# Two transformer blocks: the first quarter of the modulation is summed by TensorE on four column tiles

## The reference

```python
mod = (c @ w_mod[l] + b_mod[l]).reshape(B, N_MOD, D)
shift_m, scale_m, gate_m = mod[:, 0, None], mod[:, 1, None], mod[:, 2, None]
...
h = rms_norm(x, g_pre_mix[l]) * (1 + scale_m) + shift_m
proj = h @ w_in[l]
```

## Time and profile before

| | us |
|---|---|
| median of 3 runs (2346.0 to 2348.29) | 2347.09 |
| the profiled execution | 2344.91 |
| its span, first to last instruction | 2343.2 |
| TensorE busy | 2323.7 |
| VectorE busy | 1672.4 |
| ScalarE busy | 1132.8 |

### The profile page before, as it was taken

How to read it: one execution, slowest core, us unless ns; L and a number is a source line. 1 busy time by engine, 2 the same in 40 slices (tenths; PEclk the granted TensorE clock), 3 DMA queues, 4 the chain that set the end, 5 groups by cost and what they waited for, 6 DMA issues and landing times.

```text
span 2343.2 us, 31060 instructions
## 1 busy us (share of the span) xinstructions
PE 2323.7 (99%) x10584; PEld 1920.3 (82%) x10584; DVE 1672.4 (71%) x2121; ACT 1132.8 (48%) x1439; POOL 450.1 (19%) x878
## 2 busy tenths in 40 slices
PE   8999999999999999999999999999999999999998
PEld 7888788887878888888888888888888888888887
DVE  6998899999876666655544466676765577888764
ACT  4544546543564444444444455444744444544654
POOL 0001001333002112112100001111121135686310
PEclk9999999999999999999999999999999999999999
DMA  9986469999957877866655657666566666665564
GB/s 391 397 321 202 156 235 372 350 345 367 361 185 253 263 252 239 271 228 200 230 195 193 193 169 233 212 219 215 183 210 216 200 212 200 198 199 190 187 210 154
DMA packets 175642, 562.62 MB, mean 240 GB/s; under 512 B 30464, under 2 KB 34848, under 8 KB 174880
## 3 DMA queue, kind: packets, MB, share of 16 engines
q1 hardware_dynamic: 145584, 528.28, 65.9%
q0 software_dynamic: 27136, 23.91, 3.5%
q10 hardware_dynamic: 2800, 8.81, 1.1%
HBM read 534.91 MB, written 2.11 MB: 229 GB/s over the span
## 4 chain that ended last, share of the span: by engine, by line
PE 92%; DVE 4%; issue 2%; DMA 1%; ACT 0%; SPq 0%; ACTq 0%; DVEq 0%
PE acc L2524 28%; PE acc L2525 28%; PE acc L2531 28%; DVE macc L1526 1%; DVE lo L1490 1%; PE tb L3111 1%; PE tb L2609 1%; DMA start_raw<-in_wa_dram 1%; PE tb L2524 1%; PE tb L2525 1%; PE tb L2531 1%; PE tb L3114 0%; PE tb L2796 0%; PE acc L2582 0%; PE acc L2584 0%
## 5 line engine op out<-in xcount | busy, mean ns | idle before, releaser
L1490 DVE TENSOR_TENSOR lo<-raw,hi 128x1024 fp32r<-128x1024 f32 x809 | 970.7, 1209 | 532.5 <-ACT hi L760 529.2
L760 ACT ACTIVATE hi<-raw 128x1024 fp32r<-128x1024 f32 x809 | 843.6, 1048 | 971.2 <-PE acc L2531 681.5
L2524 PE MATMUL acc<-hi,Hh 128*128 128x512 f32 x1928 | 759.9, 394 | 1.1 <-issue 0.9
L2525 PE MATMUL acc<-hi,Hl 128*128 128x512 f32 x1928 | 751.0, 390 | 0.0
L2531 PE MATMUL acc<-lo,Hh 128*128 128x512 f32 x1928 | 515.8, 389 | 1.1 <-DVE lo L1490 1.1
L2524 PEld LDWEIGHTS acc<-hi,Hh 128*128 128x128 f32 x1928 | 362.1, 188 | 78.3 <-issue 4.0
L2531 PEld LDWEIGHTS acc<-lo,Hh 128*128 128x128 f32 x1928 | 361.9, 188 | 77.2 <-DVE lo L1490 1.6
L2525 PEld LDWEIGHTS acc<-hi,Hl 128*128 128x128 f32 x1928 | 362.2, 188 | 74.9 <-issue 1.4
L2524 PE MATMUL acc<-hi,hbh 128*128 128x512 f32 x512 | 202.7, 396 | 0.0
L2525 PE MATMUL acc<-hi,hbl 128*128 128x512 f32 x512 | 199.6, 390 | 0.0
L675 POOL DMA_DIRECT2D tok<-sgt x176 | 86.2, 498 | 495.1 <-DVE sgt L1616 381.5
(11 more groups left out here) (398 smaller groups left out, 2336.1 us busy)
## 6 DMA issues: line engine op xcount, KB each, us to landing
raw<-in_wa_dram SPq DMA_DIRECT2D x680, 512.0 KB, 4.4
late_raw<-in_wa_dram SPq DMA_DIRECT2D x96, 512.0 KB, 6.3
raw<-in_wb_dram SPq DMA_DIRECT2D x96, 512.0 KB, 4.2
start_raw<-in_wa_dram SPq DMA_DIRECT2D x64, 512.0 KB, 7.6
raw<-in_wc_dram SPq DMA_DIRECT2D x64, 512.0 KB, 4.2
tok<-sgt POOLq DMA_DIRECT2D x416, 32.0 KB, 4.5
landed<-sgt POOLq DMA_DIRECT2D x192, 32.0 KB, 4.0
pt_landed<-att_parts POOLq DMA_DIRECT2D x192, 12.0 KB, 3.0
```

Of the source, the lines that this page charges most:

```text
L760: act.activation(hi[:, s, 0:n], raw[:, r, 0:n], ACT.Copy).then_inc(hi_ready, 1)
L1490: dve.tensor_tensor(lo[:, s, 0:n], raw[:, r, 0:n], hi[:, s, 0:n].bitcast(F32), ALU.subtract)\
L2524: pe.matmul(dst(tt), a, hi[:, s, w], start=first and i == 0, stop=False)
L2525: pe.matmul(dst(tt), b, hi[:, s, w], start=False, stop=False)
```

## The change

TensorE sums tiles 0 to 7, 12, 14 and 15 itself. It uses its array as four column tiles of 32 columns: the stationary operand of each is one column of c spread over 32, the moving operand four blocks of 32 columns of the raw tile, and the result gathers in one bank of `tb`, repeated on 32 partitions of each quarter. One 128x128 transpose by VectorE brings it into the wanted layout. VectorE keeps tiles 8 to 11 and 13 and hands its sum in `macc` to TensorE, which adds it into the same bank. VectorE also norms the second half of the tokens and copies half of the turned blocks, which ScalarE did. The fillers before the first tile fall from 76 to 34, and those before the fourth unit from 20 to 8. Unit 3 is multiplied unsplit too, from the scaled slices in `sgt`. The second quarter's tiles are requested from unit 6 instead of unit 4. ScalarE asks for the tables after the scaling for the third quarter. Semaphores become one for each column tile or sender.

```diff
-START_PE = (5, 8)
-FIRST_UNITS = 3
+START_PE = tuple(range(8)) + (12, 14, 15)
+QUADRANTS = 4
+FIRST_UNITS = 4
+TURN_BANKS = 0, 1, 2, 0, 1, 2, 2, 2
...
+HALF_SUMS = HALF_TILES, START_PE.index(KD - 1) + 2
...
-START_LEAD, START_LAST = 4, 16
+START_LEAD, START_LAST = 6, 16
...
-                        sp.wait_ge(mod_summed, START_PE.index(free_of) + 1)
+                        for j in range(QUADRANTS):
+                            sp.wait_ge(mod_summed[j], START_PE.index(free_of) + 1)
...
-            for unit in range(FIRST_UNITS):
+            for unit in range(FIRST_UNITS - 1):
                 load(wa[RING_MODS + unit])
                 load_start(HALF_TILES + unit)
...
             for n in (slice(0, D // 2), slice(D // 2, D)):
-                for tt in range(TT):
-                    act.activation(xn[:, tt, n], x[:, tt, n], ACT.Copy, scale=rstd[:, tt:tt + 1]).then_inc(start_normed, 1)
-            for k in range(KD // 2):
...
+                act.activation(xn[:, 0, n], x[:, 0, n], ACT.Copy, scale=rstd[:, 0:1]).then_inc(start_normed[0], 1)
+            for k in range(0, 6, 2):
...
-            split_to(RING)
+            for b in range(3):
+                act.wait_ge(tb_free[b], 1 + TURN_BANKS.count(b))
             scale_second()
-            at = P
-            for dst, n in ((ropeC, TT * HD), (ropeS, TT * HD), (iropeC, TT * IROPE), (iropeS, TT * IROPE)):
-                act.dma_start(dst[:], table_in[:, at:at + n].rearrange("p (a b) -> p a b", a=TT)).then_inc(const_in, 16)
-                at += n
-            act.dma_start(mask1[:], mask1_in).then_inc(const_in, 16)
...
             split_to(2 * PHASE - 1)
             scale_in(2)
...
+            def start_turned(k):
+
+                dve.wait_ge(tr_copy, k + 1)
+                dve.tensor_copy(xnT[:, 2 * k:2 * k + 2, :], tb[:, TURN_BANKS[k], :].rearrange("p (k t) -> p k t", k=2))\
+                    .then_inc(tb_free[TURN_BANKS[k]], 1)
...
             def start_pair_input(i):
...
-                dve.wait_ge(mod_based, i + 1)
-                dve.wait_ge(mod_read, 2 + i + 1)
-                ins = dve.tensor_tensor(pair(modfm[:, 0:8]), pair(tb[:, 3, 0:8]), pair(modfm[:, 0:8]), ALU.add)
-                ins.then_inc(mod_taken, 1)
+                sums = macc[:, 0, i * P:(i + 1) * P]
+                for j in range(QUADRANTS):
+                    dve.wait_ge(mod_summed[j], HALF_SUMS[i])
+                chain(dve.transpose(sums, tb[:, 3, T + i * P:T + (i + 1) * P]))
+                dve.tensor_tensor(pair(modfm[:, 0:8]), sums.rearrange("p (s k r) -> p s k r", s=2, r=32)[:, :, :, 0],
+                                  pair(vec("b_mod", 0, 8)), ALU.add).then_inc(mod_taken, 1)
...
+            def start_second():
+
+                for j in range(2, 4):
+                    dve.tensor_scalar(h_now[:, j, :], xnT[:, j, :], fA[:, j:j + 1], modfm[:, 4 + j:5 + j], ALU.mult, ALU.add)\
+                        .then_inc(start_scaled[1], 1)
+                dve.wait_ge(start_scaled[1], 2)
+                dve.wait_ge(in_hi, 2)
+                dve.tensor_tensor(Hl[:, 2:4, :], h_now[:, 2:4, :], Hh[:, 2:4, :].bitcast(F32), ALU.subtract).then_inc(in_split, 1)
...
             dve.wait_ge(fm_loaded, 16)
-            for m in range(HALF_TILES):
-                if m not in START_PE:
-                    start_rows(m)
-                if m == 0:
-                    dve.wait_ge(ssq_ready, c.up("ssq"))
-                    rms(D)
...
+            dve.wait_ge(ssq_ready, c.up("ssq"))
+            rms(D)
+            for n in (slice(0, D // 2), slice(D // 2, D)):
+                dve.tensor_scalar(xn[:, 1, n], x[:, 1, n], rstd[:, 1:2], None, ALU.mult).then_inc(start_normed[1], 1)
+            for k in (1, 3, 5):
+                start_turned(k)
             start_pair_input(0)
+            start_turned(6)
...
             for m in range(HALF_TILES, KD):
                 if m not in START_PE:
                     start_rows(m)
-                if m == HALF_TILES + 2:
-                    start_base(1)
-            dve.wait_ge(in_hi, 1)
-            dve.tensor_tensor(Hl[:, 0:2, :], xnT[:, 0:2, :], Hh[:, 0:2, :].bitcast(F32), ALU.subtract).then_inc(in_split, 1)
-            split_to(RING)
+                if m == HALF_TILES + 1:
+                    start_turned(7)
+                if m == HALF_TILES + 3:
+                    dve.wait_ge(in_hi, 1)
+                    dve.tensor_tensor(Hl[:, 0:2, :], xnT[:, 0:2, :], Hh[:, 0:2, :].bitcast(F32), ALU.subtract).then_inc(in_split, 1)
...
             start_pair_input(1)
-            start_pair(1)
+            start_second()
...
+            def column_sums(half, src, gain, first, last):
+
+                blocks = src.rearrange("p (i f) -> p i f", f=P)
+                at = slice(T + half * P, T + (half + 1) * P)
+                for j in range(QUADRANTS):
+                    quadrant = slice(32 * j, 32 * j + 32)
+                    ins = pe.matmul(tb[quadrant, 3, at].rearrange("p (i r) -> p i r", r=32), gain.to_broadcast([P, 32]),
+                                    blocks[:, :, quadrant], start=first, stop=last, tile_position=(0, 32 * j))
+                    yield j, ins
...
             def sum_rows(m):
...
+                for r in range(2):
+                    for j, ins in column_sums(half, start_raw[s][:, r * N:(r + 1) * N], vec("c", m % HALF_TILES * 2 + r),
+                                              m in (0, START_PE[HALF_TILES]) and r == 0, m in (HALF_TILES - 1, KD - 1) and r == 1):
+                        if r == 1:
+                            ins.then_inc(mod_summed[j], 1)
+
+            def sum_second():
+
+                pe.wait_ge(mod_used, start_used(KD))
+                for j, ins in column_sums(1, macc[:, 0, N:], ones[:], False, False):
+                    ins.then_inc(mod_summed[j], 1)
...
-            turn_ident(76)
+            turn_ident(34)
             pe.wait_ge(fm_loaded, 16)
...
+            for m in range(3):
+                sum_rows(m)
+                turn_ident(4)
+            for k in range(3):
+                turn_xn(k)
+            for m in range(3, 6):
+                sum_rows(m)
+                turn_xn(m)
+            sum_rows(6)
+            turn_ident(4)
+            sum_rows(7)
+            turn_xn(6)
...
-            for dst in (lambda tt: tb[:, tt, :], *first_parts):
-                unsplit_unit(dst)
-            pe.wait_ge(mod_based, 2)
-            sum_half(1)
-            for _ in range(20):
+            unsplit_unit(latent_parts, lambda k: xnT[:, k, :], start_scaled[0], True)
+            turn_xn(7)
+            unsplit_unit(first_parts[0], lambda k: xnT[:, k, :], start_scaled[0], True)
+            unsplit_unit(first_parts[1], lambda k: xnT[:, k, :], start_scaled[0], True)
+            fill(2)
+            sum_rows(12)
+            sum_rows(14)
+            sum_second()
+            sum_rows(15)
+            for _ in range(8):
                 pe.transpose(tb[:, 2, 0:P], ident[:], ident[:])
+            unsplit_unit(latent_parts, lambda k: sgt[:].rearrange("p t (k n) -> p (t k) n", k=2)[:, 2 + k, :], start_scaled[1], False)
             pe.wait_ge(in_split, 2)
-            latent_unit(0, 1)
             for dst in first_parts:
                 unit(dst, Hh, Hl, 2, 2, N, False, True)
```

More of the change, by code:

```diff
@@ L364, in two_blocks @@
         mod_used = sem("mod_used")
-        mod_summed = sem("mod_summed")
-        mod_based = sem("mod_based")
-        start_normed = sem("start_normed")
-        start_scaled = sem("start_scaled")
+        mod_summed = [sem(f"mod_summed{j}") for j in range(QUADRANTS)]
+        start_normed = [sem(f"start_normed{tt}") for tt in range(TT)]
+        start_scaled = [sem(f"start_scaled{i}") for i in range(2)]
         memory_set = sem("memory_set")
@@ L584, in _ @@
                 load_start(m)
-            for unit in range(FIRST_UNITS):
+            for unit in range(FIRST_UNITS - 1):
                 load(wa[RING_MODS + unit])
                 load_start(HALF_TILES + unit)
-            for m in range(HALF_TILES + FIRST_UNITS, KD):
+            for m in range(HALF_TILES + FIRST_UNITS - 1, KD):
                 load_start(m)
-            for unit in range(FIRST_UNITS, FFN0):
+            for unit in range(FIRST_UNITS - 1, FFN0):
                 for q, kt in START_AT.get(unit, ()):
@@ L925, in _ @@
             scale_in(2)
+            at = P
+            for dst, n in ((ropeC, TT * HD), (ropeS, TT * HD), (iropeC, TT * IROPE), (iropeS, TT * IROPE)):
+                act.dma_start(dst[:], table_in[:, at:at + n].rearrange("p (a b) -> p a b", a=TT)).then_inc(const_in, 16)
+                at += n
+            act.dma_start(mask1[:], mask1_in).then_inc(const_in, 16)
             split_to(3 * PHASE - 1)
@@ L1676, in start_rows @@
             def start_rows(m):
-                half, s = m // HALF_TILES, m % START_SLOTS
-                dst = macc[:, 0, half * N:(half + 1) * N]
-                first = m == (0, HALF_TILES + 1)[half]
+                s = m % START_SLOTS
```

(42 more changed lines are left out.)

43 lines of the change are left out of this document (17 added, 26 removed).

## The result

The changed kernel takes 2352.19 us (median of 11 runs, 2349.64 to 2353.8) against 2345.82 for the kernel before beside it (11 runs): ratio 1.0027, 95% interval 1.0019 to 1.0035. It is slower by 6.4 us, outside the range of 2342.3 to 2349. The profiled execution took 2351.61 us with a span of 2349.8.

What follows compares the result with a forecast made beforehand. TensorE, busy 99% of the span, was taken as the bound. Restart -4.9 plus 0.7 for the unsplit unit gave -4.1, plus 1.2 given back to DMA -2.9: median 2344.2 us, range 2342.3 to 2349.

Steps and rivals of the forecast that it cites:

- (a): First quarter's start: TensorE sums tiles 0 to 7 at 0.6 us each, unsplit units start at 22.0 instead of 25.04.
- (b): First quarter's second half: tiles 12, 14, 15 on TensorE; it resumes at 36.4 instead of 41.29, 4.9 us earlier.
- (c): Fourth unit unsplit: 3.44 us against 2.72 gives back 0.7; fifth unit begins 4.1 us earlier than 44.0.
- (d): DMA up to unit 19: it lands 1.0 us earlier, so TensorE can be 2.9 us early, not 4.1.
- The prediction's path, the chain behind unit 19's landing: hi, four scalings, Hh, Hl after unit 19 lands: 5.37 us, ending at 82.55, limits TensorE to 2.9 early.
- (e): Late table requests near 131 us hold ScalarE 2.2 us; cost to TensorE taken as nothing, at most 0.5 without cover.
- serial: Rival: the four column tiles run one after another, 1.80 us a tile, 2355.6 us; chance 0.12.
- half-way column tiles: Rival: 0.8 to 1.25 us per sum tile, 2346.4 us (2344.2 to 2349.3); chance 0.16.
- DMA does not cap: Rival: a shallower DMA queue lets all of 4.1 us and some 0.3 more stay, 2342.7 us; chance 0.08.
- the tables or the idle fillers bite: Rival: slower TensorE clock at the units' start or missed splits at unit 38 cost 1.5 to 3 us, 2346.5; chance 0.10.

Runs made afterwards that it cites:

- e5: Changed kernel with the second quarter's tiles loaded with their first 512 columns only; 2347.73 us, ratio 1.0014.
- e3: Changed kernel with START_LEAD back at 4; 2349.7 us, ratio 1.0019.
- e2: Kernel before with only the table requests moved behind the third quarter's scaling; 2346.91 us, ratio 1.0011.
- e11: Changed kernel plus instructions nobody waits for (TensorE 74, VectorE 18, ScalarE 8, SyncE 106) to realign code; 0.3 us below the expected 2348 to 2348.7.
- e8: Kernel before with 182 more TensorE instructions that nobody waits for, from unit 20 on; 2348.65 us, ratio 1.0015.
- e9: Kernel before with 256 more TensorE instructions that nobody waits for, from unit 20 on; 2346.67 us, ratio 1.0006.
- e4: Changed kernel with START_LEAD 4 and each table requested behind one of units 25 to 29; 2348.05 us, ratio 1.0013.
- e12: e4 with the four added-instruction alignments of e11; 1.3 us under the kernel before.

## Why the prediction was wrong

(a) and (b) held: 0.64 us a tile against 0.6, resumption at 36.95 against 36.4. Of the bounds, 0.45 to 1.80 us, the column tiles stand at the low end. The factor of the Trainium skill, TensorE: Matmul & The Clock Gate, Part 3, would have made it an estimated 0.76; the trace, 0.64, is nearer to the 0.6 of four at once. The drain on a change of tiling mode of which the Trainium skill speaks, TensorEngine Tiling (Array Packing), Key Properties, is, if there is one here, inside the 1.2 us from one sum to the next with four transposes between. (c) held: the fifth unit starts 3.9 us earlier, against 4.1.

(d) failed in its size. The step was "The engines lose 0.2 (0 to 0.8)", from two transfers still under way at 39.9, until 41.8. There were two, and they landed at 40.9 and 42.1, but they filled only a small part of the engines: the share is 0.14 in 40 to 41 us. Behind the last request, at 34.03, the engines stayed full for 5.9 us; the next one came after 6.6, at 40.66 instead of 39.9, and they were full again only 2.3 us behind it. The window's 236 instead of 401 GB/s in 5 us is (401 - 236)/401 x 5 = 2.1 us. That DMA caps the lead up to unit 19 is shown by e5, and the size by the landing: forecast 1.0 us earlier, measured 1.4 later (79.61 against 78.20), of which the hole accounts for 1.9 and 0.5 has no name. e3 has no hole and starts unit 19 at 77.15, where the forecast had 77.2. I had counted the transfers still under way rightly, and took them to keep all engines full to the end. At TensorE the miss is larger: 0.7 and 0.2 us late at 99 us in the two traces, where -2.9 was forecast. The prediction's path, the chain behind unit 19's landing, isn't what held it: TensorE's last wait there, for z, ends at 77.46, before unit 19 lands. It had lost its lead by then, in four waits behind late units.

(e) failed. The step was "I take nothing", since TensorE comes to the lo of unit 38 only at 139.55. I looked for slack at TensorE's next product; there is some. But the resource without slack is VectorE, which works through 140 to 170 us with no gap and paces TensorE from 150 on. What starts it 3.6 us late is late at the end of that stretch. The estimate of 2.2 us "if ScalarE's next hi is late as well" was the right size: measured 1.5 (e2) to 2.9.

The step that was missing is the code's place. The sum priced what the instructions do, not that 182 of them displace every later piece of TensorE's program, and that the other engines' programs are displaced too. It put this term at nothing, without a reason. By e11 it is worth 3.4 us by means and 4.0 by medians; the two traces of the changed kernel lose 2.5 and 2.8 us behind 521. So it is about as large as the misses in (d), 3.1 to 3.6, and (e), 2.9, and which of the three is the largest isn't shown. The Trainium skill, Runtime: NRT & Kernel Launch, Instruction fetch mechanics, says that programs are fetched in blocks of 16 KiB (256 instructions) through a DMA queue of the engine's own, at a cost "mostly hidden". The size agrees with the q8 rows (0.02 MB and near 256 records from one piece to the next); the pieces of q14, 8 KB, do not agree with it. Hidden the cost is most of the time; by e8 against e9 it isn't always, and the traces show one load that is late with it.

The rivals: serial or half-way column tiles did not happen; "DMA does not cap" is refuted; the one nearest was "the tables or the idle fillers bite", right in its first half, with 1.5 to 3 us for the misses at unit 38, and given 0.10.

What stays open. Why the piece at 2140 us takes 2.2 us in the changed kernel and others 1.0, and by what path a piece makes a load late, isn't shown. The place doesn't cost the same in every execution: e3 has the code of the changed kernel at its displaced place, and its one trace loses only 0.3 us behind 521. The runs do not say which engine's pieces matter beside TensorE's; SyncE's, ScalarE's and VectorE's were only moved together. Between 521 and 700 us the same kernel can differ by 1.4 us from one execution to the next (before and before again), so e4's and e12's losses there in a single trace are not explained. Falls of the clock came in 8 of the 16 traces that followed the first: twice at 25 us with the start of the kernel before, five times at 76 to 80 us in versions of the changed kernel, once at 560 us. Each follows a short wait (0.1 to 1.8 us), but most waits of this length are followed by none.

## What to carry to other kernels

Before pricing a stall as hidden, find the engine that has no idle time in the next 30 us: delay on it is kept, whoever is waiting at the moment. When a load in a shared queue gets a later condition, compare how long the engines stay full behind the last request with how long the queue stops; the last transfers under way need not fill them. And when an edit shifts the program of a kernel that is bound by just-in-time transfers, compare it with a version padded to the same place before judging the edit by a fifth of a per cent or less.

## What was unexpected of the hardware

A 16 KB piece of code took between 0.9 and 2.2 us on the DMA engine that carried it, in the middle of the weights' transfers. A load of 512 KB that was under way with it took 5.6 us (after) and 6.1 (e8) instead of 3.5 (before). Instructions added only to move the place of these pieces moved a kernel of 2345 us by 2.4 us (e8 against e9) to 3.9 us (e12 against e4).

TensorE's clock fell to half for 3.4 us in the middle of a stretch in which TensorE was never idle for more than 1.8 us at a time. In the changed kernel it came at 560 us, behind a wait of 1.8 us for lo:

```profile
555.00:560.00 5.00, 3.23 (x17) 2.38 (x15) 4.97 (x6) 1.94 (x3) 2.99 (x7) 1.00 0.65 246
560.00:565.00 5.00, 5.00 (x17) 3.93 (x16) 5.00 (x6) 1.92 (x2) 4.85 (x10) 0.66 0.96 324
```

So a short wait can cost its own length and 1.7 us more. And one of ScalarE's five table requests held it for 1.50 us, where the others took 0.34 to 0.45; only the sum of five in a row was expected.
